# Modulation pieces in the even layer's last column groups, a staggered down projection, and norm sums and weight splits in another order

## What is computed

```python
mod = jnp.einsum('bd,ldm->lbm', jax.nn.silu(c), w_mod) + b_mod[:, None, :]
for i in range(DEPTH):                       # DEPTH = 2
    sh_m, sc_m, g_m, sh_f, sc_f, g_f = [t[:, None, :] for t in jnp.split(mod[i], 6, axis=-1)]
    h = x * (1.0 + sc_m) + sh_m
    y = even_mixer(...) if i % 2 == 0 else odd_mixer(...)
    x = layer_norm(ALPHA * x + (1.0 + g_m) * y, ln_mix_g[i], ln_mix_b[i])
    h = x * (1.0 + sc_f) + sh_f
    y = swiglu(h, w_gate[i], w_up[i], w_down[i])     # 1024 -> 2816 -> 1024
    x = layer_norm(ALPHA * x + (1.0 + g_f) * y, ln_ffn_g[i], ln_ffn_b[i])
```

## Time and profile before

| | before |
|---|---|
| median of three runs | 1158.64 us |
| profiled execution, its own time | 1160.85 us |
| its span | 1159.5 us |
| mean granted TensorE clock | 0.996 |
| TensorE busy | 98% of the span |
| VectorE busy | 72% |
| ScalarE busy | 54% |
| GpSimd busy | 8% |
| HBM read | 229.56 MB, 199 GB/s over the span |

### The profile page before, as it was taken

The page is one execution under the profiler, slowest core; times in us unless marked ns, Lnnn a source line. Parts: engine busy times, 40 slices in busy tenths (PEclk is TensorE's granted clock), DMA queues, the critical chain, the costliest instruction groups (busy, mean ns, idle before and its releaser), DMA issues.

```text
span 1159.5 us, 24992 instructions
## 1 busy us (share of the span) xinstructions
PE 1131.2 (98%) x10542; PEld 1081.8 (93%) x10542; DVE 839.9 (72%) x1427; ACT 628.7 (54%) x1075; POOL 87.1 (8%) x101
## 2 busy tenths in 40 slices
PE   8999889999999999999999999999999999999998
PEld 6997779999998999989999999999999999999987
DVE  5689579987986788797665569768655667676643
ACT  3467446544444677666544454744655557555542
POOL 3000013000000200113000014400000000000000
PEclk9999999999999999999999999999999999999999
DMA  9963757998997644546756542744245553655550
GB/s 314 382 227 116 280 181 227 295 320 278 338 308 254 205 146 146 183 146 213 223 183 198 189 158 74 254 148 147 74 146 182 182 187 123 209 176 197 185 179 37
DMA packets 194688, 232.22 MB, mean 200 GB/s; under 512 B 4084, under 2 KB 169556, under 8 KB 194577
## 3 DMA queue, kind: packets, MB, share of 16 engines
q1 hardware_dynamic: 193984, 230.32, 59.9%
q0 software_dynamic: 592, 0.31, 0.2%
HBM read 229.56 MB, written 1.05 MB: 199 GB/s over the span
## 4 chain that ended last, share of the span: by engine, by line
PE 83%; DVE 8%; DMA 4%; ACT 2%; issue 2%; POOL 0%; SPq 0%; DVEq 0%; ACTq 0%
PE ps L154 81%; DVE wlo L187 3%; PE ps L157 2%; DMA raw<-in_w_up_dram 2%; DMA XR<-in_x_dram 1%; DVE hL L196 1%; DMA MW<-in_w_mod_dram 1%; DVE T L187 1%; ACT whi L166 1%; DMA raw<-in_w_in_even_dram 1%; DVE LT L187 1%; DVE LT L196 0%; DVE Fg L196 0%; DVE T L196 0%; POOL T L187 0%
## 5 line engine op out<-in xcount | busy, mean ns | idle before, releaser
L187 DVE TENSOR_TENSOR wlo<-raw,whi 128x1024 fp32r<-128x1024 f32 (+1 forms) x346 | 411.0, 1209 | 171.2 <-ACT whi L166 169.0
L154 PE MATMUL ps<-hH,whi 128*128 128x256 f32 (+3 forms) x1792 | 515.4, 288 | 1.0 <-DVE hL L196 0.7
L154 PE MATMUL ps<-hH,wlo 128*128 128x256 f32 (+3 forms) x1792 | 504.4, 281 | 3.0 <-DVE wlo L187 3.0
L154 PE MATMUL ps<-hL,whi 128*128 128x256 f32 (+3 forms) x1792 | 504.3, 281 | 0.0
L166 ACT ACTIVATE whi<-raw 128x1024 fp32r<-128x1024 f32 (+1 forms) x346 | 349.7, 1033 | 206.5 <-PE ps L154 132.9
L154 PEld LDWEIGHTS ps<-hH,whi 128*128 128x128 f32 x1792 | 337.3, 188 | 6.8 <-issue 3.5
L154 PEld LDWEIGHTS ps<-hH,wlo 128*128 128x128 f32 x1792 | 337.5, 188 | 4.0 <-DVE wlo L187 4.0
L154 PEld LDWEIGHTS ps<-hL,whi 128*128 128x128 f32 x1792 | 337.8, 188 | 0.3
L154 PE MATMUL ps<-uL,whi 128*128 128x256 f32 x352 | 99.2, 282 | 0.0
L154 PE MATMUL ps<-uH,whi 128*128 128x256 f32 x352 | 99.0, 281 | 0.0
L154 PE MATMUL ps<-uH,wlo 128*128 128x256 f32 x352 | 98.4, 279 | 0.0
(11 more groups left out here) (314 smaller groups left out, 1630.8 us busy)
## 6 DMA issues: line engine op xcount, KB each, us to landing
MW<-in_w_mod_dram SPq DMA_DIRECT2D x47, 1024.0 KB, 6.5
raw<-in_w_up_dram SPq DMA_DIRECT2D x44, 1024.0 KB, 5.5
raw<-in_w_in_dram SPq DMA_DIRECT2D x36, 1024.0 KB, 5.0
raw<-in_w_down_dram SPq DMA_DIRECT2D x27, 1024.0 KB, 5.6
raw<-in_w_gate_dram SPq DMA_DIRECT2D x22, 1024.0 KB, 7.3
raw<-in_w_in_odd_dram SPq DMA_DIRECT2D x12, 1024.0 KB, 5.2
raw<-in_w_in_even_dram SPq DMA_DIRECT2D x8, 1024.0 KB, 9.3
raw<-in_w_down_dram SPq DMA_DIRECT2D x8, 768.0 KB, 6.8
```

The source lines that it names most:

```text
L154: return self.queued(self.e.matmul(out, lhsT, rhs, start=start, stop=stop, skip_group_check=True, **kw), length if pos is None else max(le ...
L187: return self.queued(self.e.tensor_tensor(out, a, b, op), 0.07 + cols(out) / self.RATE)
```

## The change

- `even`: `k.mods_soon` is set to 8 after the first run of columns, to 10 before the second `rows` group, to 14 before the third column group and to 18 before the fourth. Before, it stays 8 until `out_small` sets it to 20.
- `out_ffn`: the last group of 256 columns is multiplied in two halves of 128 into banks 5 and 1. For the first two weight slots both halves go side by side; for the third slot all 18 matmuls of output 6 come first, then the 18 of output 7.
- `layer_norm`: block 6 is now added to acc and sqa in all norms, and four sum matmuls remain in each. They are planned when both partial sums are due, and in the norms after the output projections 0.5 us after that. In the norm with `early=False` (after layer 0's down projection) `k.sums_first` keeps wanted pieces back until the last sum is queued.
- `normalized`: the four products with rstd are no longer queued in one go; between them the planner may queue other work, weight splits among it.

```diff
@@ turn
-    if needed and k.quiet < 3 or idle and not k.summing and (needed or k.mods_queued not in BY_VECTOR):
+    if needed and k.quiet < 3 and not k.sums_first or idle and not k.summing and (needed or k.mods_queued not in BY_VECTOR):
         k.mods.go(now)
@@ even
+    k.mods_soon = 8
     k.act.table(SET_EXP)
...
     start(k, by_dve(k, rows(k, 2, rest[0]), 2, m.VS[:, :, 0:256], k.v, 0))
+    k.mods_soon = 10
     start(k, by_act(k, rows(k, 1, rest[1]), 1, m.VS[:, :, 256:512], 1.0, k.v, 1))
+    k.mods_soon = 14
     for i, b in enumerate((0, 2)):
+        if i:
+            k.mods_soon = 18
         k.rope_jobs.append((blocks(k, (b,), rest[2 + i], TOK), b, m.RD[:, 4 + 2 * i:6 + 2 * i, :], 0.125, 2 + i))
@@ out_ffn
-    for j in range(4):
-        b = (2, 4, 0, 1)[j]
+    for j in range(3):
+        b = (2, 4, 0)[j]
...
+    fill_next(k, 5, 1)
+    jobs = [[(m.ps[(5, 1)[n]][:, 0:S], slot, slice(n * 128, n * 128 + 128), True) for n in range(2)] for slot in slots[3]]
+    for i in range(2):
+        for ks in (range(4), range(4, 8)):
+            multiply(k, jobs[i], ks, u, 8 * i, s, k.u_low, (i, ks.start) == (0, 0), False, False, (ks.start // 4,))
+    for n in range(2):
+        for ks in (range(4), range(4, 6)):
+            k.quiet = 3 if (n, ks.start) == (1, 4) else 0
+            y = multiply(k, [jobs[2][n]], ks, u, 16, s, k.u_low, False, ks.start == 4, False, (ks.start // 4,) if n else ())
+        k.y[6 + n] = y
@@ layer_norm
     k.hold = k.summing = True
+    k.sums_first = not early
...
-    if where[6][0] == where[7][0]:
-        pe.wait_ge(*td[6]).mm(mean, ones[:, 0, :], T(6), True, False)
-        yield due(squared[6])
-        pe.wait_ge(*squared[6]).mm(var, ones[:, 0, :], sq[6], True, False)
-    else:
-        part = dve.settle().tt(acc, acc, T(6), ALU.add).inc()
-        total = pool.wait_ge(*squared[6]).settle().tt(sqa, sqa, sq[6], ALU.add).inc()
-        yield due(part)
-    alone = where[6][0] != where[7][0]
-    pe.wait_ge(*part).mm(mean, ones[:, 0, :], acc, alone, False)
-    yield due(total)
-    pe.wait_ge(*total).mm(var, ones[:, 0, :], sqa, alone, False)
+    part = dve.settle().tt(acc, acc, T(6), ALU.add).inc()
+    total = pool.wait_ge(*squared[6]).settle().tt(sqa, sqa, sq[6], ALU.add).inc()
+    yield due(part, total) + (0.5 if to is not None and early else 0.0)
+    pe.wait_ge(*part).mm(mean, ones[:, 0, :], acc, True, False)
+    pe.wait_ge(*total).mm(var, ones[:, 0, :], sqa, True, False)
...
-    k.summing = False
+    k.summing = k.sums_first = False
@@ normalized
-    dve.settle().wait_ge(*k.rstd)
+    dve.settle()
     for i in range(4):
+        yield max(k.pe.clock + 0.01, dve.clock - 0.1)
+        dve.settle().wait_ge(*k.rstd)
         done = dve.tt(f[i], f[i], rstd, ALU.mult)
@@ program
-        wide = [((2, 4, 0, 1)[j // 2], j % 2 * S) for j in range(KD)]
+        wide = [((2, 4, 0)[j // 2], j % 2 * S) for j in range(6)] + [(5, 0), (1, 0)]
```

## The result

The changed kernel took **1141.55 us** (median of 4 runs, 1141.23 to 1144.01) against 1158.04 before: ratio **0.9861, 95% interval 0.9847 to 0.9875**. The predicted 1148.1 and its range from 1143.5 to 1156.0 both lie above it. The direction was right, and so were the signs that the prediction had named for the trace; the size was not: about 16 us went, not 10.5. The profiled execution was again a long one of its kernel, 1144.01 us.

A forecast was written before the change was run, and what follows sets the result against it. TensorE, busy 98% of the span, was taken as the bound; -5.6 - 2.2 - 0.9 - 0.8 - 1.0 = -10.5 from 1160.85 gave 1150.35, and 2.2 lower for the median 1148.1 us, range 1143.5 to 1156.0.

The forecast's parts named there:

- the signs that the prediction had named for the trace: In the changed trace: dense-stage pieces waiting at most 1 us, no clock drop near 123, four sums per down norm.
- Part one, the 11.0 us that can go: Even layer: spreading modulation pieces removes 7.2 us of waits and half clock in the attention, 3.8 in the norm behind.
- Part one, the 5.4 us given back: Even layer: 3.6 us returns to the attention chain, 1.2 to weight waits in the dense stage, 0.6 to the norm.
- my second rival: Even layer's attention: TensorE and chain mesh better, half the give-back stays, more if pieces 20 and 21 fit: 1145.4, 12%.
- The base of the sum: Whole kernel: -10.5 us set against the profiled 1160.85, giving 1150.35, then 2.2 lower for the runs' median: 1148.1.
- Part two, -3.1: Down projection norms: staggered columns and sums ahead of pieces save 2.2 us in layer 0 and 0.9 in layer 1.
- I take none: Before the odd layer's projection: TensorE stands about 1.8 us in two parts, assumed to bring no clock drop.
- The -0.7: Layer 0's down norm: the gain, instead of -2.2 us, if the thinly used stretch draws the clock drop again.
- Part three, -0.8: Layer 1 norm: later sums cut TensorE's wait at the first sum from 1.20 to 0.4 us; bounds -1.2 and 0.
- Part four, -1.0: Gate and up projections: splits between normalizing products remove waits of 0.43, 0.70 and 0.2 us; bounds -1.6 and +0.5.
- The first rival: Even layer's attention: the chain, not TensorE, sets the stage's end, so spreading pieces gives nothing: -4.9, 1153.7 us, 22%.
- The third: Dense stage: pieces wait for weights behind raw loads, from about 8 us between issue and landing: +14.1, 1162.2 us, 7%.

The follow-up runs named there:

- part one alone: Kernel before with only the `k.mods_soon` settings of 10, 14 and 18 in `even` added: ratio 0.9946 to the kernel before.
- part four undone: Changed kernel with the four products with rstd queued in a row again: ratio 0.9900 to the kernel before.
- parts three and four alone: Kernel before with only the sums after both partial sums plus 0.5 us in the two small norms, and splits between the normalizing products: ratio 0.9976 to before.
- parts one and two together: Kernel before with the `k.mods_soon` settings, the staggered down projection and sums ahead of pieces, without the 0.5 us or splits between products: ratio 0.9893 to before.
- part two alone: Kernel before with only the staggered last down projection columns and sums ahead of pieces: ratio 0.9972 to the kernel before.
- Twelve rounds: Changed kernel with twelve rounds of selection in place of eight, 6.2 us more on VectorE: ratio 0.9931 to the kernel before.

## Why the prediction was wrong

Split by clock, the prediction's -10.5 was -7.9 of work and waits and -2.6 of clock (1.6 in the attention, 1.0 before the odd layer). Measured: -13.8 and -1.8. At full clock the parts taken alone exceed my terms by 2.5 us (part one), 1.5 (part two) and 1.2 (parts three and four), and all four together by 0.7 more, which is within the uncertainty; the clock gave 0.8 less than I had.

- **Part one, the 11.0 us that can go:** right. The waits and the half clock of rows 5 and 7 in the attention and the norm's gap of rows 8 are gone; in their stead there are two waits of 0.7 and 0.3 us.
- **Part one, the 5.4 us given back: this step failed.** "Two bounds that close never mesh wholly: I give back 3.6" had no row that gave its size. In the changed kernel TensorE stands 1.1 us in the attention where I had 3.6, 0.2 at the norm's first sum where I had 0.6, and not at all for weights in the dense stage where I had 1.2: 1.3 for 5.4. In part one alone it is 0.9 in the attention, 0.6 at the sum, 0.5 for a split behind it and 0.76 for a piece in the odd layer, 2.7 together. That fits the runs: 11.0 less the 1.6 of clock and less 2.7 is 6.7 at full clock, measured 6.5, where I had 4.0. Undone in the changed kernel it costs 6.7 too, 1.4 less than 9.4 less the 1.3 of waits there; that is within the uncertainty of two such differences. Both ends of the stage lie later than I had them, since pieces 20 and 21 now run inside the attention (143.64 and 146.41, 2.2 us), beside the 1.1 of waits: the last oL ends at 147.0, not 141.8, and the second pass starts at 147.4, where TensorE's work alone was to end at 144.3. What I missed is that the first pass of the output projection needs none of the chain's last results and fills its holes. Halving it costs 3.0 us. It is my second rival that happened, pieces 20 and 21 included.
- **The base of the sum.** I set the 11.0 us against the profiled execution and then took off the 2.2 us by which this exceeded the median. These are partly the same microseconds: that execution had two drops of the clock, which 26 of 44 did not. It is likely most of the reason why part one is 9.5 us between traces and 6.3 by the ratio. On the whole change the two errors nearly cancel, since the changed kernel's profiled execution was as long beside its own median.
- **Part two, -3.1:** the right size, with the wrong composition. At full clock it is 3.0 to 3.6, where I had 2.1 (why it is more isn't shown); the clock's 1.0 doesn't come by it alone. "I take none" of the drop was wrong for both profiled executions of the changed kernel, whose clock fell behind 1.88 us, and right, by their readings of 0.999 and 1.000, for the six others. The Trainium skill ("TensorE: Matmul & The Clock Gate", Part 1), which warns against leaving TensorE to wait, was the better guide to those two. The -0.7 that I had worked out for that case was too pessimistic.
- **Part three, -0.8:** 1.1 in the trace, 0.8 by the runs. As predicted, though by the runs it can't be told from nothing.
- **Part four, -1.0: mis-sized.** 1.5 in layer 1 and 0.7 to 1.4 in layer 0, 3.5 by the runs. I counted 1.1 in layer 1 and 0.2 in layer 0, from the waits of rows 12 as they stood. With part one in, layer 0's wait is 0.5 (part one alone) or 0.70 (part four undone) instead of 0.2; a row of before can't show that. My worry was that the slowdown beside GpSimd would move along with its products. The Trainium skill ("GPSIMD Engine Reference", section 1) names the shared SBUF interfaces; the slow splits before agree with that, but here one of eight was slow, and TensorE didn't wait for it.
- **The clock.** I gave each drop a place and a part. The runs show it as a chance: 2.7 us lost on average before, 2.3 to 2.9 with part one, part two or parts three and four alone, 0.9 in the changed kernel and with parts one and two together. Why each alone saves almost nothing is open. The profiled execution of part two alone had three drops, that of parts three and four alone none, though it stood 1.48, 1.15 and 2.29 us in the same places; one profiled execution of each can't settle it.
- **The first rival**, the chain as the end of the stage, was 1 to 3.5 us away. Twelve rounds show its price. **The third** didn't come: loads took up to 8.8 us from issue to landing, above my threshold of 8, but the planner placed the pieces behind them, and only one waited, 0.3 us.

What remains open is 1 us or so in the hybrid, where kernels with the same code differ by standing still that the profile puts down to no releaser, once 0.97 us in the changed kernel, once 0.66 before:

```profile
754.62 0.62 PE L154 MATMUL ps<-Qg,Kg 128*32 128x16 f32 x41 [0.97 <-issue]
```

## What to carry to other kernels

When waits on the bounding engine are taken away, don't discount the gain by a guess because a second chain is near: look for work on the bounding engine that needs nothing from that chain, and ask whether the change lets it fall into the chain's holes. Take the fluctuation of the granted clock out of every comparison (time x clock, averaged over the runs) before parts are weighed, and don't subtract an execution's excess from a gain that may contain it. In a kernel whose order a planner makes, an edit that moves the planner's clock is two edits; put the clock back to see the one you mean.

## What the runs showed of the hardware

- A drop of the granted clock doesn't need one long gap. Behind gaps of 0.93, 0.71 and 0.51 us within 3 us it fell for 6.8 us; behind one of 2.09 at 122.35 it didn't fall, and behind one of 1.41 at 168.60 it did, in the same execution. In part two alone it fell at 169.95, behind gaps of 1.05, 0.74, 0.35 and 0.71 us from 163.7 on; in the kernel before the same four gaps, to within 0.01 us, had no drop behind them. My reading of before, that gaps up to 1.20 are harmless, was a coincidence of few cases.
- It is a chance between executions of one program: the changed kernel read 1.000 in four of eight, 0.999 in two and 0.998 in two, with 1141.1 to 1144.1 us.
- With four matmuls of ones in the gap of 1.88 us the clock was 1.00 there in both profiled executions, and with the order kept they had no cost that can be measured. Without them it fell in 8 of 11 profiled executions with the same gap.
- VectorE's 128x1024 subtraction (a split) took 1.75 us in three of the five cases of the kernel before in which GpSimd's products ran, and 1.21 in the other two.
